# Rotating the expert slots: scatter after the next slot's first gate and up products

## The reference, cut to what matters

```python
def hier_moe(x, w_grp, b_grp, w_exp, b_exp, w_gate, w_up, w_down):
    pg = softmax(xs @ w_grp + b_grp); g_sel = argmax(pg); g_prob = max(pg)
    le = (xs @ w_exp + b_exp) of the chosen group
    top_p, top_i = top_k(softmax(le), 2); top_p = top_p / sum(top_p)
    gate = one_hot(g_sel * 4 + top_i) * g_prob * top_p, summed over the two
    hdn = silu(xs @ w_gate[e]) * (xs @ w_up[e]) * gate[e]
    return sum over e of hdn @ w_down[e]
```

## Time and profile before

| | us |
|---|---|
| median of 3 runs | 2325.72 (2320.05 to 2325.89) |
| the profiled execution | 2326.32 |
| its span, first to last instruction | 2324.3 |
| PE busy | 2120.3 (91%) |
| PEld (weight loads) busy | 1902.1 (82%) |
| DVE busy | 1518.1 (65%) |
| ACT busy | 1175.1 (51%) |
| mean granted TensorE clock | 0.957 |

### The profile page before, as it was taken

The page is one execution under the profiler, slowest core; times in us unless marked ns, Lnnn a source line. Parts: engine busy times, 40 slices in busy tenths (PEclk is TensorE's granted clock), DMA queues, the critical chain, the costliest instruction groups (busy, mean ns, idle before and its releaser), DMA issues.

```text
span 2324.3 us, 36380 instructions
## 1 busy us (share of the span) xinstructions
PE 2120.3 (91%) x13978; PEld 1902.1 (82%) x13978; DVE 1518.1 (65%) x2263; ACT 1175.1 (51%) x1665; POOL 75.1 (3%) x55
## 2 busy tenths in 40 slices
PE   7998987999999989889999888799999887999997
PEld 6998966899999978779998866588777756778876
DVE  5556668656566644466664455689887355888885
ACT  4443443543344335454433344577776354676774
POOL 1000024000000020000000000000000000000000
PEclk9999998899999999999999979899999999999998
DMA  8545240445544523334564412399995513799991
GB/s 278 203 165 162 92 162 1 163 163 190 189 163 162 186 85 128 128 104 168 173 205 121 156 37 80 122 328 331 336 314 189 208 37 109 249 314 329 314 354 48
DMA packets 312309, 421.07 MB, mean 181 GB/s; under 512 B 7844, under 2 KB 266304, under 8 KB 312096
## 3 DMA queue, kind: packets, MB, share of 16 engines
q1 hardware_dynamic: 308864, 415.93, 52.7%
q10 hardware_dynamic: 2816, 2.38, 0.5%
q0 software_dynamic: 544, 1.62, 0.2%
HBM read 416.69 MB, written 1.05 MB: 180 GB/s over the span
## 4 chain that ended last, share of the span: by engine, by line
PE 82%; DVE 10%; ACT 4%; issue 2%; DMA 1%; ACTq 1%; POOL 0%; DVEq 0%; SPq 0%
PE banks L553 11%; PE banks L554 11%; PE banks L555 11%; PE banks L2507 7%; PE banks L2509 7%; PE banks L2508 7%; PE banks L805 5%; PE banks L806 5%; PE banks L807 5%; PE banks L2502 2%; PE banks L2561 1%; DVE w_lo L2776 1%; DVE pieces L871 1%; PE banks L1299 1%; DVE arena L1201 1%
## 5 line engine op out<-in xcount | busy, mean ns | idle before, releaser
L2776 DVE TENSOR_TENSOR w_lo<-weight_ring,w_hi 128x1024 fp32r<-128x1024 f32 x384 | 450.1, 1220 | 55.2 <-ACT w_hi L2621 51.8
L553 PE MATMUL banks<-x_hi,w_hi 128*128 128x256 f32 x1408 | 400.7, 285 | 8.6 <-DVE w_lo L506 7.9
L554 PE MATMUL banks<-x_lo,w_hi 128*128 128x256 f32 x1408 | 399.2, 284 | 0.0
L555 PE MATMUL banks<-x_hi,w_lo 128*128 128x256 f32 x1408 | 399.1, 283 | 0.0
L2621 ACT ACTIVATE w_hi<-weight_ring 128x1024 fp32r<-128x1024 f32 x384 | 381.5, 1052 | 33.3 <-PE banks L2509 33.3
L499 ACT ACTIVATE w_hi<-weight_ring 128x1024 fp32r<-128x1024 f32 x88 | 93.0, 1057 | 418.5 <-PE banks L555 418.3
L871 DVE TENSOR_TENSOR pieces<-weight_ring,pieces 128x512 fp32r<-128x512 f32 (+2 forms) x245 | 165.4, 687 | 199.6 <-ACT pieces L860 198.0
L553 PEld LDWEIGHTS banks<-x_hi,w_hi 128*128 128x128 f32 x1408 | 271.0, 192 | 11.0 <-DVE w_lo L506 8.7
L554 PEld LDWEIGHTS banks<-x_lo,w_hi 128*128 128x128 f32 x1408 | 271.1, 193 | 0.1
L555 PEld LDWEIGHTS banks<-x_hi,w_lo 128*128 128x128 f32 x1408 | 271.0, 192 | 0.0
L860 ACT ACTIVATE pieces<-weight_ring 128x512 fp32r<-128x512 f32 (+2 forms) x245 | 150.8, 627 | 235.4 <-PE banks L807 222.0
(11 more groups left out here) (390 smaller groups left out, 3988.6 us busy)
## 6 DMA issues: line engine op xcount, KB each, us to landing
weight_ring<-in_ffn_w_in SPq DMA_DIRECT2D x88, 1024.0 KB, 7.6
weight_ring<-in_moe_w_gate SPq DMA_DIRECT2D x64, 1024.0 KB, 6.8
weight_ring<-in_moe_w_up SPq DMA_DIRECT2D x64, 1024.0 KB, 9.3
weight_ring<-in_moe_w_down SPq DMA_DIRECT2D x64, 1024.0 KB, 11.3
weight_ring<-in_ffn_w_out SPq DMA_DIRECT2D x44, 1024.0 KB, 9.7
weight_ring<-in_hg_w_in SPq DMA_DIRECT2D x12, 1024.0 KB, 8.2
weight_ring<-in_fox_w_in SPq DMA_DIRECT2D x12, 1024.0 KB, 8.5
weight_ring<-in_nsa_w_in SPq DMA_DIRECT2D x10, 1024.0 KB, 7.9
```

The lines of the kernel that those rows point to most:

```text
L553: pe.matmul(out, w_hi, m_hi, start=start, stop=False, skip_group_check=True)
L554: pe.matmul(out, w_hi, m_lo, start=False, stop=False, skip_group_check=True)
L555: return pe.matmul(out, w_lo, m_hi, start=False, stop=stop, skip_group_check=True)
L2776: dve.tensor_tensor(self.piece(s, p, self.w_lo), self.piece(s, p), self.piece(s, p, self.w_hi.bitcast(F32)), ALU.subtract).then_inc(sem[ki ...
```

## The change

Three things move, and nothing is added to or removed from the computation.

1. TensorE: the gate and up products of step 0 (`pe_first`) are made ahead of the loop for the first slot, and for each following slot between the last down products and the scatter (`pe_scatter`) of the slot before. A branch on `i + 1 < count` decides, so that the code of the scatter stands twice in the body.
2. TensorE, at the layer's start: the gates product, with the read of `count`, comes behind step 0's products of the first slot.
3. ScalarE and VectorE: pieces 0 and 1 of step 1 are made ahead of the loop (ScalarE: behind the copy of the gates; VectorE: behind its wait for that copy), and in each slot's end for the next slot (VectorE: ahead of the residual adds).

```diff
@@ pe
         self.pe_gather(pe, 0)
+        for n in ("st0", "st1", "st2"):
+            b.wait_read(pe, name + n)
+        self.pe_first(pe, self.step0, 2 * self.gather0 + 2)
         count = self.load_plan(pe)
         pe.wait_ge(sem["gates"], self.layer + 1)
...
         b.filled(last, name + "gates")
-        for n in ("st0", "st1", "st2", "gates"):
-            b.wait_read(pe, name + n)
+        b.wait_read(pe, name + "gates")
@@ pe_slot
-        pe.wait_ge(sem["xs_lo"], i * 2 + (2 * self.gather0 + 2))
-        for s in range(self.STEPS):
+        for s in range(1, self.STEPS):
...
         self.pe_turn(pe, end, self.step(i, end))
         self.pe_gather(pe, i + 1)
         self.pe_down(pe, end, self.step(i, end))
-
-        pe.wait_ge(sem["xs_lo"], i * 2 + (2 * self.gather0 + 4))
+        with pe.If(i + 1 < count):
+            self.pe_first(pe, self.step(i + 1, 0), i * 2 + (2 * self.gather0 + 4))
+            self.pe_scatter(pe, i)
+        with pe.If(i + 1 >= count):
+            pe.wait_ge(sem["xs_lo"], i * 2 + (2 * self.gather0 + 4))
+            self.pe_scatter(pe, i)
+
+    def pe_first(self, pe, n, tokens):
+        pe.wait_ge(self.sem["xs_lo"], tokens)
+        pe.wait_ge(self.sem["hidden"], n + 1)
+        for p in range(4):
+            self.pe_gate_up(pe, 0, p, n)
+
+    def pe_scatter(self, pe, i):
+        k, sem = self.k, self.sem
         pe.wait_ge(sem["y_ready"], i * 2 + (2 * self.slot0 + 2))
@@ act
         b.read(act.activation(self.gates, src, ACT.Copy), name + "gates")
+        self.act_second(act, 0, self.step0 + 1)
         self.slots(act, count, self.act_slot, self.act_skip)
+
+    def act_second(self, act, i, n):
+        self.wait_full(act, 1, i)
+        for p in range(2):
+            self.act_piece(act, 1, p, n)
@@ act_slot
-                self.act_piece(act, s, p, self.step(i, s))
+                if s > 1 or p >= 2:
+                    self.act_piece(act, s, p, self.step(i, s))
@@ act_end
             for p in (2, 3):
                 self.act_piece(act, 0, p, self.step(i + 1, 0))
+            self.act_second(act, i + 1, self.step(i + 1, 1))
@@ dve_route
         self.dve_tokens(dve, 0)
         b.wait_read(dve, name + "gates")
+        for p in range(2):
+            self.dve_piece(dve, 1, p, self.step0 + 1)
@@ dve_slot
-                self.dve_piece(dve, s, p, self.step(i, s))
+                if s > 1 or p >= 2:
+                    self.dve_piece(dve, s, p, self.step(i, s))
@@ dve_end
             dve.wait_ge(sem["gu_lo"], self.step(i + 1, 0) * 4 + 4)
             self.dve_release(dve, 0)
+            for p in range(2):
+                self.dve_piece(dve, 1, p, self.step(i + 1, 1))
```

More of the change, by code:

```diff
@@ L2547, in pe_slot @@
                 self.pe_gate_up(pe, s, p, self.step(i, s))
-                if s and p == 1:
+                if p == 1:
                     if s == 1:
@@ L2551, in pe_slot @@
                     self.pe_turn(pe, s - 1, self.step(i, s - 1))
-            if s:
-                self.pe_down(pe, s - 1, self.step(i, s - 1))
+            self.pe_down(pe, s - 1, self.step(i, s - 1))
         self.pe_turn(pe, end, self.step(i, end))
```

## The result

The changed kernel takes 2330.72 us (median of 10 runs, 2325.08 to 2333.73) against 2323.36 for the kernel before (10 runs, 2320.05 to 2326.12): the ratio is 1.003, 95% interval 1.0019 to 1.004. It is slower by about 7 us, with an interval from 4.4 to 9.3. The profiled execution took 2331.98.

What follows compares the result with a forecast made beforehand. A slot was taken as TensorE's work plus a few holes, with VectorE nearly full. Slot ends -4.7 and layer starts +6.6 gave +1.9 on 2326.3, 2328.2; with the median 0.6 lower, 2328.0 was predicted, range 2320 to 2337.

Steps and rivals of the forecast that it cites:

- the bound at which I set "slower": Whole kernel: a change counts as slower beyond about 0.3%, 7 us; the chance given to slower was 0.24.
- The hole before the scatter goes, 0.4 comes before piece 2: Slot end, TensorE: the 1.15 us hole before the scatter goes and a 0.4 us wait for step 0's piece 2 comes.
- The gain at a slot's end is 0.8: Six slot ends: the next slot's first `pe_down` comes 0.8 us earlier, 4.7 us over six.
- The layer's start costs 3.3: Start of both layers: 4.0 lost plus 0.2 for branches minus 0.9 for the clock, 3.3 us each, 6.6 in all.
- half of the gain from the slow stretch in step 0: Layer's start, TensorE: losing step 0's slow-clock stretch would gain 1.75 us; half was taken, 0.9.
- rival C: Layer's start, slower: the clock falls behind the gates product and slows work into `pe_down`; +7.2 us, 2333.5, chance 0.08.
- The order on ScalarE: Layer's start: gates' copy, two pieces and silu queue behind step 0 and the gates product; first `pe_down` 4.0 us later.
- ScalarE's load, 1.28, in line at the start: First slot, ScalarE: silu's table load of 1.28 us follows the two pieces, with no extra 1.38 us drain.
- rival B: Slot ends, slower: TensorE's branches lie in the open, 0.77 us at eight ends; +8.1 us, 2334, chance 0.16.
- Fill 1 lands in time: Slot end: weights for ScalarE's earlier piece 0 of step 1 land 1.6 us before they are read, costing nothing.
- Rival A: Faster: VectorE is no bound at slot ends and the start's slow clock goes; -7.2 us, 2319, chance 0.10.
- the 10.5 us in a row on VectorE: Slot end: from the scatter's start, adds, `hidden`, pieces and `h_lo` need 10.5 us in a row, TensorE 9.4.

Runs made afterwards that it cites:

- Run 6: Changed kernel with silu's two waits swapped and VectorE's gate copy, `hidden` and piece 2 of step 1 ahead of the adds; ratio to the kernel before 0.9978.
- run 2: Changed kernel with ScalarE's and VectorE's pieces 0 and 1 of step 1 ahead of the gates' copy or the wait for it; ratio to the kernel before 1.0006.
- run 5: Changed kernel with silu's wait for `hidden` put ahead of its wait for `gu_used`, nothing else; ratio to the kernel before 1.0027.
- run 3: Changed kernel's layer start alone: at slot ends the scatter precedes step 0 again and pieces of step 1 follow the adds; ratio to the kernel before 1.0073.
- run 4: The kernel of run 3 with silu's wait for `hidden` put ahead of its wait for `gu_used`; ratio to the kernel before 1.0022.
- run 1: Changed kernel with the gates product back ahead of step 0, the wait for ScalarE's gates copy staying behind step 0; ratio to the kernel before 1.0000.
- run 8: Changed kernel's slot end alone: TensorE's layer start as before, with gates product, waits for its copy, then step 0; ratio to the kernel before 1.0000.
- run 7: Changed kernel with the edits of run 1, run 4 and Run 6 together; 2307.25 us against 2323.6 for the kernel before, ratio 0.9933.

## Why the prediction came out as it did

The forecast was +1.9 by the profile, "no change", 2328; the measured 2330.7 lies in the range, above the point, just over the bound at which I set "slower". The time flatters the forecast. The kernel before took 2323.4 in the runs beside it and not the 2325.7 that I had started from, so the change cost 7.4 us (4.4 to 9.3), and +1.9 lies outside of that. The signs and places of both parts were right. One size was not, and 2.4 us stay without a place.

- *The hole before the scatter goes, 0.4 comes before piece 2.* Right: 1.15 is gone, and the new wait is 0.34 (1571.62 to 1571.96).
- *The gain at a slot's end is 0.8.* The mis-sized term: 0.25 (1.5 over six, so 3.2 of the 5.5 us that the forecast was short). I had put `hidden` 0.3 after the last add, and it came 0.85 after it (1579.19 to 1580.04); in this slot's end that is all that is missing, as the other differences cancel (the scatter 0.1 later than I had it, the adds 0.1 shorter, and from `hidden` to `pe_down` 5.74 against 5.75). The 0.3 was for the gate copy alone. In the kernel before the adds run packed, and the gate copy follows them at once (they end at 1570.56):

```profile
1570.48 0.15 DVE L2796 TENSOR_TENSOR wide<-wide,consts 128x4 f32<-128x4 f32 x1
```

Now each add waits for its bank, and so the sequencer stands at the last wait until 1578.50. The chain of waits of the changed kernel shows what it still has to do from there: start us, us, what (DVEq is VectorE's sequencer; L2430 is the loop, L2431 its branch for a used slot, L2433 that for a skipped one).

```profile
1578.50 0.08 DVE x_res L2868
...
1578.74 0.06 DVEq L2433
...
1579.09 0.29 issue
...
1579.45 0.05 DVEq L2431
...
1579.67 0.18 DVE wide L2821
...
1580.04 0.08 DVE hidden L2808
...
1580.46 4.62 DVE w_lo L2801 x4
...
1585.22 0.44 DVE h_lo L2814
...
1585.78 0.49 PE banks L2509
```

From 1578.50 to 1579.67 the branches and register instructions of the slot's end and the loop's entry pass one by one; the add covers 0.69 of it and 0.48 is in the open; the gate copy and the wait behind it take the other 0.37 of the 0.85. I had charged such an entry to VectorE only at the layer's start. Run 6 takes the whole queue off the path and gets 1.6 us a slot.
- *The layer's start costs 3.3.* Measured 3.39 and 3.17, but the sum was right by two errors that cancel. I had taken half of the gain from the slow stretch in step 0. It went entirely (5.56 instead of 7.20, 0.7 more than I took), and came back in step 1 (8.5 from 1500.58 to 1509.04, where 5.7 is the work). I had held that it would be hidden there, since TensorE would wait for VectorE. It was not: `h_lo` was ready at 1508.02, and TensorE came to `pe_down` 1.0 later, so 0.9 of it was in the open (silu to `pe_down` 7.59, forecast 6.70). So part of rival C's mechanism was there, and that the two cancel is luck. The order on ScalarE, silu behind a copy behind a product behind step 0, was right, and run 2 shows it. It was put at 4.0 to 4.2; run 2 gives back 2.5, and what stays is the gates product's own place: step 1 waits for its copy and then meets the slow clock.
- *ScalarE's load, 1.28, in line at the start.* Right (1500.16), and with no drain around it: silu stands at 1501.45, 0.01 behind its end. The Trainium skill (ScalarE: Activation LUTs, What ACT_TABLE_LOAD costs) would have a further 1.38; this trace doesn't agree. What I didn't see is that the load also changed its place against silu's wait, now that the loop begins with silu. In the changed kernel it costs nothing (run 5); where the slot's end is not held up by the adds, it costs 1.3 a slot (runs 3 and 4), and at the starts of runs 1 and 8 1.4.
- *The branches are hidden on TensorE (rival B).* Right for TensorE. But the same branches are in the open on VectorE, which is what the term above lacked.
- *Fill 1 lands in time.* Right: ScalarE's piece of step 1 starts without a wait for a DMA.
- *Rival A* fell as argued: the 10.5 us in a row on VectorE bound; they were 10.9 (1574.85 to 1585.78).

Open: the stretches that the change touches account for +5.0 of the measured 7.4 (interval 4.4 to 9.3). Whether the other 2.4 are drift I can't settle; the rest of the span varied from 1820 to 1830 us between the profiled executions. The sums of the stretches lie inside the interval of the whole in runs 2 to 7. In runs 1 and 8 they don't (-4.0 against 0.0 with 3 to either side; -2.7 against -2.6 to +2.8): there the whole is some 3 to 4 us longer than the stretches say, and no run shows where.

Open too: no run changes the pause ahead of step 0 or step 1 and nothing else, so what makes the granted clock fall is not shown, only beside what it fell.

## What to carry to other kernels

When work is moved ahead of a wait on one engine, look at what stands in the other engines' programs behind their waits for the moved piece: both losses here were queues in the larger part, silu behind the gates' copy (2.5 of 4.6 a layer) and `hidden` behind the adds. Look also at what covers a loop's branches: behind four packed adds VectorE's gate copy followed at once (1570.48), and when the same adds waited one by one, 0.48 us of the loop's entry came into the open ahead of it. And judge a rotated loop by stretches between marks as well as by the whole, and say where the two differ: here the medians carried some 3 us to either side, and in two of eight runs they didn't show what the stretches did.

## What the runs showed of the hardware

A table load stands where the program puts it against the two waits of its activation: with the late wait ahead of it, its 1.28 us lie on the path (run 3: load at 1575.95, silu at 1577.25); with the late wait behind it, they don't (run 4: load at 1575.52, silu at 1577.16, 0.35 after the load, when step 0 has ended). Swapping two `wait_ge` lines is worth 8.1 us in six slots (runs 3 and 4).

The granted clock, in both layers of each run: 20 tiny products in 2.3 us and 2.6 us of standing still were followed by a stretch at half clock (granted 0.50) even though 5.6 us of dense products at full clock came right before them. The same products and 0.8 or 1.0 us of standing still were followed by a shorter slow stretch (run 2, step 1 to `pe_down` at 0.78; before, step 0 at 0.76). With 0.5 us of standing still or none there was no slow stretch (runs 8, 1 and 7, step 0 at 1.00). Pauses of 1.1 us between dense products, at the slot ends, were followed by none either, nor were 1.7 us behind the gather's products (changed kernel, step 0 at 1.00).
